# Two-block transformer kernel on one core: stick-breaking outputs kept features first, both output norms applied as per-token factors in the output product, and half units between the attention's iterations

## The chip, the cores and the metric

The kernel runs on one core of one Trainium2 chip. The metric is the device time of one execution in microseconds (us), lower is better. The engines that matter are TensorE (PE in the profile; PEld are its weight loads), VectorE (DVE) and ScalarE (ACT). SyncE (SP) issues the weight transfers.

## The reference, cut to what matters

`x` has 512 tokens of width 1024. A first block mixes and feeds forward, then a second block (three attentions, gates, 16 experts) follows, which the change doesn't touch. The part of the first block that it touches:

```
u = rms_norm(x, norm_mix) @ w_in           # 2560 columns: lru_x, lru_g, q, k, v of 512 each
y_lru = gelu(lru_g) * rg_lru(conv(lru_x))  # [512 tokens, 512 features]
# stick-breaking attention, 8 heads of 64, query blocks of 128:
z = q @ k.T / 8;  mask = key < query
att = where(mask, exp(log_sigmoid(z) + suffix sums of log_sigmoid(-z)), 0)
y_att = att @ v                            # [512, 512]
y = concat(rms_norm(y_lru, norm_lru_out), rms_norm(y_att, norm_att_out))
x = x + y @ w_out                          # w_out [1024, 1024]
h2 = rms_norm(x, norm_ffn) ...             # the feed-forward follows
```

`rms_norm(y, g)` is `y * rsqrt(mean over the 512 features of y*y + 1e-6) * g`: a factor per token and a gain per feature.

## The kernel before, in words

`plan` is a list of steps, written in Python before anything is emitted. Every engine walks the same list and emits its share of each step, so the list's order is the order of each engine's queue, and semaphores count finished steps.

A weight product is a *unit*. SP loads 1 MB of weights into one half of `RAW`; ACT rounds them to `WH` (L1161), DVE takes the remainder to `WL` (L1342), each for unit u+1 while unit u is at work, and PE forms three products (hi*hi, lo*hi, hi*lo) for each of 8 (or 4) slices of the contraction. Such a product has one record in the trace. Units of mode "F" give features first (128 features by 512 tokens; L1643 to L1645), "T" tokens first (L1660 to L1662), "wide" 512 columns of output for four token tiles (L1651 to L1653). Their results go to the banks `LIN`; while attention runs, to two of them in turn, and a product into the second of the two waits for the sigmoids of the iteration it stands in (`e_ab`). ACT or DVE evacuates. `out_half(j, h)` is a wide unit: columns 512*j of `w_out`, rows of the LRU half (h=0) or of the attention half (h=1), 4 slices, four results, each added to `X` by DVE.

The attention "stick" has 16 iterations (4 pairs of heads by 4 query blocks). With i counted from 0, iteration i of a pair has 4, 3, 2, 1 key tiles for i mod 4 = 0, 1, 2, 3. The order in iteration i:

- S(i): two score products into PSUM (L1690); ACT takes two sigmoids of each (`SK`, `SE`, L1203 and L1204, four instructions).
- W(i): DVE masks the last tile of `SE`, scans `SK` along the keys, multiplies into `PB` (L1396, L1397, L1403).
- T(i-1): PE transposes `PB` (L1773). It waits for W(i-1), and for the copies C(i-2).
- C(i-1): ACT and DVE copy the transposes into `PT` (L1314, L1584; DVE has a share only with 3 or 4 key tiles). It waits for O(i-2), since `PT` is single.
- O(i-2): PE multiplies by the values into the bank `PV` (L1792): `PT` is the stationary operand, 64 columns of `VT` move. DVE copies `PV` into `YT`, tokens first (L1437).
- fill(i): whatever the table `fill` has for i, whole units above all.

S(i) sits ahead of T(i-1) on PE, so what PE has to do between S(i) and T(i) is T(i-1), O(i-2), fill(i) and S(i+1).

The norm of `y_lru` (features first, `YL_`) is spread over the attention: `lsquare` (ACT squares), `lnorm` (PE sums the squares with a matrix of ones, L1755, which gives every token's sum on all 128 partitions; ACT takes the root, L1284; DVE the reciprocal of 128 x 512, L1566, and the product with `YL_`, L1567), `lsplit` (the gain and the split into `XH`, `XL`, L1289 and L1573). A root needs another activation table than a sigmoid, so tables are loaded ahead of it and behind it. The norm of `y_att` comes after the attention: `rms` on `YT` (ACT squares with sums, L1247; root; DVE reciprocal and scaling, L1512), PE transposes (L1739), ACT and DVE apply the gain and split (L1233, L1501). `out_half(1, 0)` covers the `rms`, and the two units of the attention half follow.

Of the kernel before, what the change touches and what calls it, by code (L numbers as in the profile page):

```python
# [85 lines left out]
def build(nc, x, w_in, w_out, w_ffn_in, w_ffn_out, mem, w_in2, w_memkv, w_branch, w_out2, w_router,  # L86
# [49 lines left out]
    YT = at("YT", R0 + 40, [P, TT, 512])  # L136
# [66 lines left out]
    def vec(c, n=1):  # L203
# [6 lines left out]
               ms_hi ms_lo saved band0 band1 x2h x2l xal lgp lgs afp af top ixp icc rcp pn ohi t1 wrp xt_ps xtA xtD lgc lg2""".split()  # L210
# [88 lines left out]
    def attention(kind, heads, halves, fill, after):  # L299
# [41 lines left out]
        def o_step(i):  # L341
            mine[i].o = add("O", dict(pv=1, o=1, ohi=int(kind != "stick")), a=mine[i])
# [33 lines left out]
    def queries(j):  # L376
        return unit(win, 1024 + UC * j, KT, "F", "scaled", dst=lambda r: QT[:, 2 * j + r, :], scale=0.125)

    def keys(j):
        return unit(win, 1536 + UC * j, KT, "F", "copy", dst=lambda r: KTT[:, 2 * j + r, :])  # L380

    def vals(j):
        return unit(win, 2048 + UC * j, KT, "T", "copy", dst=lambda r: VT[:, 2 * r:2 * r + 2, UC * j:UC * j + UC])
# [10 lines left out]
    def norm_sum():  # L394
        st = add("lnorm", dict(res=1, evA=1, yn=1), after=qkv[1], who=["act"], r0=len(results))
        take_banks(st)

    def out_half(j, h):
        return unit(w_out[0], 512 * j, 4, "wide", "accX", src=("xl", "xa")[h], row0=512 * h)
# [119 lines left out]
    SRC = {"x": (XH, XL), "xl": (XH[:, 0:4], XL[:, 0:4]), "xa": (XH[:, 4:8], XL[:, 4:8]), "m": (MH, ML), "a": (AH, AL), "y0": (YH2, YL2), "y1": (YH3, YL3),  # L519
# [625 lines left out]
    def _(act):  # L1145
# [73 lines left out]
        for st in plan:  # L1219
# [14 lines left out]
            elif k == "rms":  # L1234
                for t in range(TT):
                    if "ready" in st.kw:
                        act.wait_ge(st.kw["ready"][t], 16)
                    elif st.src is YT:
                        wait(act, "o", st.at)
                    else:  # L1240
                        wait(act, "evD", st.at, TT - 1 - t)
                    if st.dst is YT:
                        dump = PB[:, t // 2, t % 2, :]
                    else:
                        dump = (XN[:, t, :] if t == TT - 1 or "ready" in st.kw else
                                (PB[:, t, :, :] if t < 2 else PT[:, :, :]).rearrange("p a b -> p (a b)"))
# [35 lines left out]
            elif k == "lnorm":  # L1282
                act.wait_ge(s["res"], st.r0 + 1)
                A(RBC[:, :], LIN[lin_of[st.r0]][:, :], ACT.Sqrt, scale=1.0 / 512, bias=eps6).then_inc(s["evA"], 1)  # L1284
                act.preload_act_table_set("sigmoid_and_others")
            elif k == "lsplit":
                act.wait_ge(s["yn"], 1)
# [28 lines left out]
            elif k == "O" and st.a.att != "stick":  # L1316
# [14 lines left out]
    def _(dve):  # L1331
# [13 lines left out]
        def evacuate(st, now):  # L1345
            for r in now.now:
# [505 lines left out]
```

## Time and profile before

| what | us |
|---|---|
| median of 3 runs | 1761.27 (1758.52 to 1764.08) |
| the profiled execution, whole | 1763.7 |
| its span, first to last instruction | 1761.5 |
| from the first score product of "stick" to the last attention output | 130.78 to 271.45 |
| from there to the last product of the attention half of `w_out` | to 307.94 |
| PE busy over the span | 1588.2 (90%) |

A row of windows reads: from:to and its length, then busy time and instructions of PE, PEld, DVE, ACT and POOL, PEclk, the share of the DMA engines and GB/s. A row of the timeline reads: start, duration, engine, line, operation, out<-in, shape, count, and in brackets how long the engine was idle before it and what ended that. An f32 matmul has two records, a product of split weights (fp32r) one: T(i) with 4 key tiles is 8 transposes. PEclk is the clock granted to TensorE in a stretch, as a share of full speed, so 0.50 is 1.2 GHz and 1.00 is 2.4 GHz.

### The profile page before, as it was taken

How to read it: one execution, taken by the hardware profiler on the slowest of the kernel's cores; microseconds unless marked ns; L12 is line 12 of the kernel's file. 1: busy time of each engine (PE TensorE's matmuls, PEld its weight loads, DVE VectorE, ACT ScalarE, POOL GpSimd, SP SyncE). 2: the span in 40 equal slices, each digit the busy share in tenths (PEclk: the TensorE clock that was granted, in tenths of full speed). 3: DMA queues.
4: the chain of work that ended last, by engine and by line, in shares of the span. 5: the costliest groups of instructions: out<-in, count | busy, mean ns of one | idle time of the engine just before them, and what ended most of it. 6: DMA issues, size and time to landing. Idle time of an engine off the chain costs nothing.

```text
span 1761.5 us, 20656 instructions
## 1 busy us (share of the span) xinstructions
PE 1588.2 (90%) x7932; PEld 1116.3 (63%) x7932; DVE 741.6 (42%) x1094; ACT 523.2 (30%) x818; POOL 112.1 (6%) x152
## 2 busy tenths in 40 slices
PE   5989799999999998998999989996699999999894
PEld 4677687887887877987667768775333534434331
DVE  4455554434334335384535444346432232322335
ACT  4253433422222223224444434222021222112211
POOL 3000000000000000031102111001500000000000
PEclk9998789999999999999999999998799999999998
DMA  6212022333332323533202112328299999999993
GB/s 196 72 52 68 25 73 72 96 96 96 94 96 93 92 81 120 144 95 97 73 28 70 48 49 72 122 94 340 81 379 416 410 418 415 415 421 417 415 418 135
DMA packets 145095, 307.90 MB, mean 175 GB/s; under 512 B 7328, under 2 KB 98848, under 8 KB 128624
## 3 DMA queue, kind: packets, MB, share of 16 engines
q1 hardware_dynamic: 138992, 294.67, 45.3%
q0 software_dynamic: 3024, 9.10, 1.6%
q10 hardware_dynamic: 2992, 2.91, 0.6%
q8 instruction: 62, 1.02, 0.2%
q14 instruction: 25, 0.20, 0.0%
HBM read 300.36 MB, written 4.56 MB: 173 GB/s over the span
## 4 chain that ended last, share of the span: by engine, by line
PE 76%; DMA 9%; DVE 8%; issue 3%; ACT 3%; ACTq 1%; SPq 0%; DVEq 0%
PE bank L1009 12%; PE bank L1643 11%; PE bank L1644 10%; PE bank L1645 10%; DMA RING<-w_gu 4%; PE bank L1651 4%; PE bank L1652 4%; PE bank L1653 4%; DMA RING<-w_down 4%; PE bank L1690 2%; PE bank L982 2%; PE bank L1773 2%; PE bank L1020 2%; PE bank L983 2%; PE bank L1660 1%
## 5 line engine op out<-in xcount | busy, mean ns | idle before, releaser
L1643 PE MATMUL bank<-XH,WH 128*128 128x512 f32 x768 | 304.9, 397 | 6.5 <-DVE WL L1342 4.5
L1644 PE MATMUL bank<-XL,WH 128*128 128x512 f32 x768 | 301.4, 392 | 0.0
L1645 PE MATMUL bank<-XH,WL 128*128 128x512 f32 x768 | 301.2, 392 | 0.0
L1342 DVE TENSOR_TENSOR WL<-RAW,WH 128x2048 fp32r<-128x2048 f32 (+1 forms) x91 | 194.1, 2133 | 152.6 <-ACT WH L1161 152.6
L1009 PE MATMUL bank<-RING,XS 128*64 128x512 f32 x488 | 222.7, 604 | 12.9 <-DMA RING<-w_gu 8.2
L1010 PE MATMUL bank<-RING,XS 128*64 128x512 f32 x496 | 226.3, 604 | 0.0
L1161 ACT ACTIVATE WH<-RAW 128x2048 fp32r<-128x2048 f32 (+1 forms) x91 | 161.8, 1778 | 151.7 <-PE bank L1653 126.4
L1643 PEld LDWEIGHTS bank<-XH,WH 128*128 128x128 f32 x768 | 145.9, 190 | 40.1 <-DVE WL L1342 5.3
L1645 PEld LDWEIGHTS bank<-XH,WL 128*128 128x128 f32 x768 | 145.7, 190 | 30.8
L1644 PEld LDWEIGHTS bank<-XL,WH 128*128 128x128 f32 x768 | 145.9, 190 | 29.8 <-issue 0.2
L1009 PEld LDWEIGHTS bank<-RING,XS 128*64 128x64 f32 x488 | 63.7, 138 | 144.4 <-issue 140.0
L1020 PE MATMUL bank<-RING,HT 128*64 128x512 f32 x512 | 118.8, 599 | 13.9 <-DMA RING<-w_down 13.7
L890 DVE TENSOR_TENSOR GUS<-bank,LOH 64x512 f32<-64x512 f32 x64 | 39.6, 675 | 136.4 <-ACT LOH L791 136.4
L791 ACT ACTIVATE LOH<-bank 64x512 f32<-64x512 f32 x64 | 32.8, 589 | 215.1 <-PE bank L1010 215.1
L879 DVE TENSOR_TENSOR X<-bank,X 128x512 f32<-128x512 f32 x64 | 44.0, 688 | 117.9 <-PE bank L983 117.9
L1020 PEld LDWEIGHTS bank<-RING,HT 128*64 128x64 f32 x512 | 34.1, 136 | 90.6 <-issue 50.0
L1364 DVE TENSOR_TENSOR X<-bank,X 128x512 f32<-128x512 f32 x72 | 49.2, 690 | 81.1 <-PE bank L1653 78.9
L1651 PE MATMUL bank<-WH,AH 128*128 128x512 f32 x176 | 69.6, 395 | 7.9 <-issue 6.9
L1660 PE MATMUL bank<-WH,XH 128*128 128x256 f32 x224 | 65.7, 293 | 8.0 <-DVE WL L1342 6.5
L1652 PE MATMUL bank<-WL,AH 128*128 128x512 f32 x176 | 69.0, 392 | 0.0
L1653 PE MATMUL bank<-WH,AL 128*128 128x512 f32 x176 | 69.0, 392 | 0.0
L1773 PE MATMUL bank<-CST,PB 128*128 128x128 f32 x304 | 49.0, 299 | 20.7 <-DVE PB L1403 16.0
(300 smaller groups left out, 2488.7 us busy)
## 6 DMA issues: line engine op xcount, KB each, us to landing
RING<-w_gu SPq DMA_DIRECT2D x123, 1024.0 KB, 13.6
RING<-w_down SPq DMA_DIRECT2D x64, 1024.0 KB, 11.8
RAW<-w_in SPq DMA_DIRECT2D x66, 512.0 KB, 4.8
RAW<-w_ffn_in SPq DMA_DIRECT2D x44, 512.0 KB, 4.7
RAW<-w_ffn_out SPq DMA_DIRECT2D x20, 512.0 KB, 4.4
RAW<-w_out SPq DMA_DIRECT2D x16, 512.0 KB, 4.6
RAW<-w_branch SPq DMA_DIRECT2D x24, 256.0 KB, 3.2
ONCE<-w_gu SPq DMA_DIRECT2D x5, 1024.0 KB, 16.2
```

Of the source, the lines that this page charges most:

```text
L1009: T.matmul(GU[b][0:CAP, :], XS[:, k - 1, 2 * i + e, :], before[:, f], start=k == 1, stop=k == 7)
L1010: ins = T.matmul(GU[b][CAP:P, :], XS[:, k, 2 * i + e, :], slot[:, f], start=k == 1, stop=k == 7)
L1020: ins = T.matmul(YB[e][h][k * CAP:k * CAP + CAP, :], HT[:, e, 2 * r + k, :], slot[:, D * k + 512 * h:D * k + 512 * h + 512], start=r == 0, ...
L1161: A(WH[:, u % 2, :n], RAW[:, u % 2, :n], ACT.Copy).then_inc(s["w_hi"], 1)
L1342: V.tensor_tensor(WL[:, u % 2, :n], RAW[:, u % 2, :n], WH[:, u % 2, :n].bitcast(F32), ALU.subtract).then_inc(s["w_lo"], 1)
L1643: T.matmul(bank[:, :st.nt], wh[:, k, c], hi, start=k == 0, stop=False)
L1644: T.matmul(bank[:, :st.nt], wh[:, k, c], lo, start=False, stop=False)
L1645: ins = T.matmul(bank[:, :st.nt], wl[:, k, c], hi, start=False, stop=k == st.K - 1)
L1651: T.matmul(bank[:, :], hi, wh[:, k, :], start=k == 0, stop=False)
L1652: T.matmul(bank[:, :], hi, wl[:, k, :], start=False, stop=False)
L1653: ins = T.matmul(bank[:, :], lo, wh[:, k, :], start=False, stop=k == st.K - 1)
L1773: ins = T.transpose(TR[kt // 2][:, c:c + P], PB[:, st.a.n % 2, j, kt * P:kt * P + P], ident)
```

## The change

- The stick attention's output product has `VT` (64 columns) as the stationary operand and 128 queries of `PT` moving, so that it comes out features first, two heads in one 128 x 128 tile. ACT squares it into `SQ`, and applies the gain of `norm_att_out` while it rounds it to `YAH`; DVE takes the remainder to `YAL`. `YT`, its `rms` and its transposes are gone.
- The sums of squares per token are products with one column of ones: `square_sum` for the attention, one per iteration, emitted behind the *next* iteration's output product; 16 of them in `lnorm` instead of four of 512 columns. A new step `asum` sums the columns behind the last iteration and makes the four factors per partition.
- `lnorm` no longer scales `YL_`; its root and reciprocal have 4 columns. The factors (`ST[:, 32:36]` and `ST[:, 36:40]`) are applied by DVE where it adds the results of `out_half` to `X`.
- The three units for the second half of q, k and v go in halves, one half per iteration 0 to 5; `memk` 0 and 1, the split, and both LRU halves of `w_out` have other places in `fill`.

```diff
     def o_step(i):
-        mine[i].o = add("O", dict(pv=1, o=1, ohi=int(kind != "stick")), a=mine[i])
+        mine[i].o = add("O", dict(pv=1, o=1, ohi=1, sq=int(kind == "stick")), a=mine[i])
...
-    fill = {0: [lambda: queries(1)], 2: [lambda: keys(1)], 4: [lambda: qkv.append(vals(1))],
-            6: [lambda: add("lsquare", dict(ysq=1), after=qkv[1])], 7: [norm_sum],
-            9: [lambda: add("lsplit", dict(yhi=4, ylo=4), after=qkv[1])], 10: [memk(0)], 12: [memk(1)],
-            14: [lambda: out_half(0, 0)]}
-    last = attention("stick", 4, 4, fill, lambda i: qkv[i // 8])
-    rms(YT, YT, 512, after=last)
-    out_half(1, 0)
-    tx(YT, XH[:, 4:8], XL[:, 4:8], 4, TT, scale=V_GATT, feeds="xa")
+    q1, k1, v1 = (halves(f(1, False)) for f in (queries, keys, vals))
+    fill = {0: [q1[0]], 1: [q1[1]], 2: [k1[0]], 3: [k1[1]], 4: [v1[0]], 5: [lambda: qkv.append(v1[1]())],
+            6: [lambda: add("lsquare", dict(ysq=1), after=qkv[1]), memk(0)], 7: [norm_sum],
+            8: [lambda: add("lsplit", dict(yhi=4, ylo=4), after=qkv[1])], 9: [memk(1)],
+            11: [lambda: out_half(0, 0)], 13: [lambda: out_half(1, 0)]}
+    stick_last = attention("stick", 4, 4, fill, lambda i: qkv[i // 8])
+    add("asum", dict(ass=1, asq=1, arc=1, rat=1), after=stick_last)
     for j in range(2):
         out_half(j, 1)
...
# ACT, step O
+                act.wait_ge(s["pv"], st.a.n + 1)
+                A(SQ[:, :], src, ACT.Square).then_inc(s["sq"], 1)
+                A(hi, src, ACT.Copy, scale=vec(V_GATT + st.a.h)).then_inc(s["ohi"], 1)
# DVE, step O
-                V.tensor_copy(YT[...], PV[...]).then_inc(s["o"], 1)
+                V.scalar_tensor_tensor(lo, src, vec(V_GATT + a.h), hi.bitcast(F32), ALU.mult,
+                                       ALU.subtract).then_inc(s["o"], 1)
# PE, step lnorm
-                for c in range(4):
-                    ins = T.matmul(LIN[lin_of[st.r0]][:, :], ones, YSQ[:, c, :], start=c == 0, stop=c == 3)
+                for t in range(TT):
+                    for c in range(4):
+                        ins = T.matmul(LIN[lin_of[st.r0]][:, t:t + 1], YSQ[:, c, t * P:t * P + P], ones[:, 0:1],
+                                       start=c == 0, stop=c == 3)
# DVE, step lnorm
-                link(V.reciprocal(RBC[:, :], RBC[:, :]))
-                V.tensor_tensor(YL_[:, :, :], YL_[:, :, :], RBC[:, :].unsqueeze(1).to_broadcast([P, 4, S]), ...)
+                V.reciprocal(ST[:, 32:36], ST[:, 32:36]).then_inc(s["lrs"], 1)
# DVE, evacuation of out_half
+                    if "part" in st.kw:
+                        dve.wait_ge(s["rat" if st.kw["part"] else "lrs"], 1)
+                        c = 32 + 4 * st.kw["part"] + r
+                        V.scalar_tensor_tensor(xs, shaped(st, bank), ST[:, c:c + 1], xs, ALU.mult, ALU.add)...
# PE, step O of "stick", behind its products
+                if a.att == "stick" and a.n:
+                    ins = square_sum(atts[a.n - 1])
                 ins.then_inc(s["pv"], 1)
```

On PE, from the sums of `lnorm` (fill 7) to the next unit. Before, the scores of iterations 8, 9 and 10 follow (512, 384 and 256 columns), with their transposes and output products between:

```order
L1755 MATMUL bank<-YSQ,CST 128x512 [waits evD,evA,ysq]
L1755 MATMUL bank<-YSQ,CST 128x512 x3
L1690 MATMUL bank<-KTT,QT 128x512 [waits tx_hi,sig,tx_lo,e_ab,evD,evA]
L1690 MATMUL bank<-KTT,QT 128x512 [waits e_ab,evD,evA]
L1773 MATMUL bank<-CST,PB 128x128 [waits tx_hi,tx_lo,ptD,sig,ptA,p]
L1773 MATMUL bank<-CST,PB 128x128
L1792 MATMUL bank<-VT,PT 128x64 [waits o,ptD,ptA]
L1792 MATMUL bank<-VT,PT 128x64 x3
```

Now the sums are 16 short products, and each output product has a product with `SQ` behind it:

```order
L1785 MATMUL bank<-CST,YSQ 128x1 [waits evD,evA,ysq]
L1785 MATMUL bank<-CST,YSQ 128x1 x15
L1713 MATMUL bank<-KTT,QT 128x512 [waits tx_hi,sig,tx_lo,e_ab,evD,evA]
L1713 MATMUL bank<-KTT,QT 128x512 [waits e_ab,evD,evA]
L1807 MATMUL bank<-CST,PB 128x128 [waits tx_hi,tx_lo,ptD,sig,ptA,p]
L1807 MATMUL bank<-CST,PB 128x128
L1822 MATMUL bank<-PT,VT 64x128 [waits o,ptD,ptA]
L1822 MATMUL bank<-PT,VT 64x128 x3
L1719 MATMUL bank<-CST,SQ 128x1 [waits sq]
```

Behind these rows both have the scores of iteration 9 and the transposes and output of 8 and 7; the next unit, `memk`, stood behind O(8) and S(10), and now stands right behind O(7).

On PE, the end of the attention. Before, the last transposes and outputs ran into the LRU unit `out_half(1, 0)`:

```order
L1773 MATMUL bank<-CST,PB 128x128
L1792 MATMUL bank<-VT,PT 128x64 [waits o,ptD,ptA]
L1792 MATMUL bank<-VT,PT 128x64 x3
L1792 MATMUL bank<-VT,PT 128x64 [waits o,ptD,ptA]
L1792 MATMUL bank<-VT,PT 128x64
L1651 MATMUL bank<-WH,XH 128x512 [waits evA,evD,tx_lo,e_ab,ylo,w_lo]
```

Now they run into `asum` and the first unit of the attention half, whose wait on `o` is the split of the last output:

```order
L1807 MATMUL bank<-CST,PB 128x128
L1822 MATMUL bank<-PT,VT 64x128 [waits o,ptD,ptA]
L1822 MATMUL bank<-PT,VT 64x128 x3
L1719 MATMUL bank<-CST,SQ 128x1 [waits sq]
L1822 MATMUL bank<-PT,VT 64x128 [waits o,ptD,ptA]
L1822 MATMUL bank<-PT,VT 64x128
L1719 MATMUL bank<-CST,SQ 128x1 [waits sq]
L1719 MATMUL bank<-CST,SQ 128x1 [waits sq,o]
L1674 MATMUL bank<-WH,YAH 128x512 [waits evA,tx_lo,evD,o,e_ab,ylo,w_lo]
```

No unit moved across the products of the attention's last iterations except `out_half(1, 0)`, which stood behind them and is now in iteration 13.

## Rows read from the trace of the kernel before

**Rows 1.** The page: busy time by engine, and the chain that ended last

```profile
PE 1588.2 (90%) x7932; PEld 1116.3 (63%) x7932; DVE 741.6 (42%) x1094; ACT 523.2 (30%) x818; POOL 112.1 (6%) x152
...
PE 76%; DMA 9%; DVE 8%; issue 3%; ACT 3%; ACTq 1%; SPq 0%; DVEq 0%
```

**Rows 2.** Windows: attention, what follows it, and 90 us of a later attention

```profile
130.78:271.21 140.43, 122.60 (x649) 101.21 (x649) 77.45 (x142) 52.51 (x101) 0.00 (x0) 0.82 0.16 53
271.21:307.94 36.73, 36.38 (x164) 29.95 (x164) 18.82 (x24) 15.56 (x23) 0.00 (x0) 0.96 0.29 87
810.00:900.00 90.00, 80.14 (x453) 59.36 (x451) 44.20 (x113) 40.71 (x96) 13.03 (x28) 0.96 0.21 62
```

**Rows 3.** Waits of PE from 130 to 308: total, times, longest

```profile
PE bank L1773 <- DVE PB L1403: 16.0, 5, 6.3
```

**Rows 4.** Windows: the stretches at the lower clock

```profile
147.90:158.10 10.20, 9.37 (x33) 8.39 (x34) 5.50 (x11) 2.40 (x2) 0.00 (x0) 0.50 0.00 0
188.80:202.50 13.70, 13.64 (x48) 10.26 (x47) 4.46 (x15) 4.95 (x8) 0.00 (x0) 0.50 0.00 0
209.30:226.40 17.10, 12.39 (x56) 11.58 (x57) 15.25 (x29) 6.70 (x12) 0.00 (x0) 0.50 0.00 0
246.90:257.10 10.20, 9.50 (x34) 8.47 (x35) 5.70 (x11) 2.40 (x2) 0.00 (x0) 0.50 0.00 0
270.80:274.20 3.40, 3.40 (x11) 2.82 (x11) 0.29 (x1) 2.39 (x8) 0.00 (x0) 0.51 0.00 0
```

**Rows 5.** Timeline of PE: waits, and what the work after them takes

```profile
150.03 3.52 PE L1792 MATMUL bank<-VT,PT 128*128 128x64 f32 x16
...
213.90 1.97 PE L1773 MATMUL bank<-CST,PB 128*128 128x128 f32 x8 [6.25 <-DVE PB L1403]
...
268.97 1.00 PE L1792 MATMUL bank<-VT,PT 128*128 128x64 f32 x8
```

**Rows 6.** Timeline of PE at the full clock: scores, transposes, a later attention's output

```profile
130.78 1.13 PE L1690 MATMUL bank<-KTT,QT 64*128 64x512 f32 x4 [1.09 <-ACT VT L1190]
143.79 1.10 PE L1773 MATMUL bank<-CST,PB 128*128 128x128 f32 x8
...
936.41 1.09 PE L1788 MATMUL bank<-PT,KVT 128*64 128x128 f32 x16
```

**Rows 7.** Windows: one F unit, one T unit, `memk`, the two last wide units

```profile
131.84:142.94 11.10, 11.10 (x50) 8.93 (x49) 6.14 (x7) 4.47 (x6) 0.00 (x0) 1.00 0.47 160
171.09:182.76 11.67, 11.67 (x98) 11.54 (x97) 6.33 (x8) 3.81 (x6) 0.00 (x0) 1.00 0.28 91
235.84:241.75 5.91, 5.91 (x48) 5.78 (x49) 5.24 (x7) 2.32 (x3) 0.00 (x0) 1.00 0.00 0
285.91:307.94 22.03, 22.03 (x98) 18.25 (x99) 11.07 (x12) 7.98 (x10) 0.00 (x0) 1.00 0.35 96
```

**Rows 8.** Line L1755 and timeline of ACT and DVE: the norm of `y_lru`

```profile
L1755 PE MATMUL bank<-YSQ,CST x8: 592/1061/1167, 197.4 to 203.0; 128*128 128x512 f32 x8
...
203.60 0.69 ACT L1284 ACTIVATE RBC<-bank,CST 128x512 f32<-128x512 f32 x1 [4.02 <-PE bank L1755]
204.31 1.28 ACT L1285 ACT_TABLE_LOAD   x1
...
204.32 3.35 DVE L1566 RECIPROCAL RBC<-RBC 128x512 f32<-128x512 f32 x1 [6.40 <-ACT RBC L1284]
```

**Rows 9.** Timelines of ACT and DVE: from S(0) to its weights

```profile
131.97 0.60 ACT L1203 ACTIVATE SK<-bank 128x512 f32<-128x512 f32 x1 [0.35 <-PE bank L1690]
...
135.82 1.27 DVE L1403 TENSOR_TENSOR PB<-SE,SC 128x512 f32<-128x512 f32 x2
```

**Rows 10.** Timelines of PE, ACT and DVE: the end of the attention and the transposes

```profile
283.65 1.91 PE L1739 MATMUL bank<-CST,YT 128*128 128x128 f32 x16
...
270.07 0.38 ACT L1314 ACTIVATE PT<-bank 128x256 f32<-128x256 f32 x1 [1.45 <-PE bank L1792]
...
271.49 0.29 DVE L1437 COPY YT<-bank 128x128 f32<-128x128 f32 x1 [1.18 <-PE bank L1792]
```

More of the change, by code:

```diff
@@ L135, in build @@
     VT = at("VT", R0 + 32, [P, TT, 512])
[L136 removed]
+    YAH = at("YAH", R0 + 40, [P, 4, S], F32R)
     FG = at("FG", R0 + 16, [P, 2, S])
@@ L374, in build, with made, queries, keys @@
     add("lgate", dict(gmm=8, sig=8), after=lgu)
[L376 to L383, printed above, removed]
+    def made(args, kw, now):
+        return unit(*args, **kw) if now else (args, kw)
+    def queries(j, now=True):
+        return made((win, 1024 + UC * j, KT, "F", "scaled"), dict(dst=lambda r: QT[:, 2 * j + r, :], scale=0.125), now)
+    def keys(j, now=True):
+        return made((win, 1536 + UC * j, KT, "F", "copy"), dict(dst=lambda r: KTT[:, 2 * j + r, :]), now)
+    def vals(j, now=True):
+        return made((win, 2048 + UC * j, KT, "T", "copy"),
+                    dict(dst=lambda r: VT[:, 2 * r:2 * r + 2, UC * j:UC * j + UC]), now)
     qkv = []
@@ L394, in norm_sum, with halves @@
     def norm_sum():
-        st = add("lnorm", dict(res=1, evA=1, yn=1), after=qkv[1], who=["act"], r0=len(results))
+        st = add("lnorm", dict(res=1, evA=1, lrs=1), after=qkv[1], who=["act"], r0=len(results))
         take_banks(st)
     def out_half(j, h):
-        return unit(w_out[0], 512 * j, 4, "wide", "accX", src=("xl", "xa")[h], row0=512 * h)
-    fill = {0: [lambda: queries(1)], 2: [lambda: keys(1)], 4: [lambda: qkv.append(vals(1))],
-            6: [lambda: add("lsquare", dict(ysq=1), after=qkv[1])], 7: [norm_sum],
-            9: [lambda: add("lsplit", dict(yhi=4, ylo=4), after=qkv[1])], 10: [memk(0)], 12: [memk(1)],
-            14: [lambda: out_half(0, 0)]}
-    last = attention("stick", 4, 4, fill, lambda i: qkv[i // 8])
-    rms(YT, YT, 512, after=last)
-    out_half(1, 0)
-    tx(YT, XH[:, 4:8], XL[:, 4:8], 4, TT, scale=V_GATT, feeds="xa")
+        return unit(w_out[0], 512 * j, 4, "wide", "accX", src=("xl", "ya")[h], row0=512 * h, part=h)
+    def halves(part):
+        return in_two(*part[0], **part[1])
+    q1, k1, v1 = (halves(f(1, False)) for f in (queries, keys, vals))
[5 more added lines that the diff above has]
+    add("asum", dict(ass=1, asq=1, arc=1, rat=1), after=stick_last)
     for j in range(2):
@@ L1283, in _ @@
                 act.wait_ge(s["res"], st.r0 + 1)
-                A(RBC[:, :], LIN[lin_of[st.r0]][:, :], ACT.Sqrt, scale=1.0 / 512, bias=eps6).then_inc(s["evA"], 1)
+                A(ST[:, 32:36], LIN[lin_of[st.r0]][:, 0:TT], ACT.Sqrt, scale=1.0 / 512, bias=eps6).then_inc(s["evA"], 1)
                 act.preload_act_table_set("sigmoid_and_others")
             elif k == "lsplit":
-                act.wait_ge(s["yn"], 1)
+                wait(act, "res", st.after.end)
                 for c in range(4):
@@ L1315, in _ @@
                 ins.then_inc(s["ptA"], 1)
-            elif k == "O" and st.a.att != "stick":
+            elif k == "asum":
+                act.wait_ge(s["asq"], 1)
+                A(ST[:, 36:40], ST[:, 124:128], ACT.Sqrt, scale=1.0 / 512, bias=eps6).then_inc(s["arc"], 1)
+            elif k == "O" and st.a.att == "stick":
+                src, hi, _ = features(st.a)
+                act.wait_ge(s["pv"], st.a.n + 1)
+                A(SQ[:, :], src, ACT.Square).then_inc(s["sq"], 1)
+                A(hi, src, ACT.Copy, scale=vec(V_GATT + st.a.h)).then_inc(s["ohi"], 1)
+            elif k == "O":
                 src, hi, _ = features(st.a)
@@ L1609, in product @@
             wait(pe, "ylo", st.at)
+            if st.src == "ya":
+                wait(pe, "o", stick_last.end)
             if st.evac == "branch":
@@ L1690, in scores, with square_sum @@
             T.matmul(o, q, kk, start=True, stop=True).then_inc(s["qk"], 1)
+        def square_sum(a):
+            c = 256 + 4 * a.h + a.qt[0]
+            pe.wait_ge(s["sq"], a.n + 1)
+            return T.matmul(PV[:, c:c + 1], SQ[:, :], ones[:, 0:1], start=True, stop=True)
         def values(a, j, kt):
@@ L1781, in _ @@
                 wait(pe, "o", st.at)
-                for kt in range(a.nkt[0] if a.att != "stick" else 0):
+                for kt in range(a.nkt[0]):
                     first, last = kt == 0, kt == a.nkt[0] - 1
```

49 lines of the change are left out of this document (25 added, 24 removed).

## Prediction

> **What bounds the kernel now.** I read the page first: PE is busy for 90% of the span and makes up 76% of the chain that ended last [rows 1]. So a change counts if it shortens PE's work, PE's idle time, or the time PE spends at the lower clock. I then read windows around the place of the change. The attention takes 140.43 us, of which PE is busy for 122.60, at a mean granted clock of 0.82; then come 36.73 us at 0.96 to the last product of `out_half(1, 1)` [rows 2]. Together that is 177.2 us, 130.78 to 307.94, and this is the stretch I redo. Next the waits: five times the transposes T wait for DVE's weights `PB`, 16.0 us in all, the longest 6.3 [rows 3]. With the start (1.1 before a bank is free, 0.8, 0.5 and 0.35 at the end, read off the timeline) PE is idle for about 18 us. Last the clock: the windows split at its changes show five stretches at the lower level, 54.6 us in all (10.2 + 13.7 + 17.1 + 10.2 + 3.4) [rows 4]. Each of the four long ones begins within two us of the start or end of a wait for `PB`, and what runs there takes about twice as long: an output product with 4 key tiles has 16 records in 3.52 us at the lower level, one with 2 tiles 8 records in 1.00 us at the full one [rows 5].
>
> **What PE has to do, at the full clock, before and after.** Per pair of heads (4, 3, 2, 1 key tiles):
>
> - Scores: 1.06 us from the start with 512 columns to the next instruction (1.13 with its tail [rows 6]), falling with the columns to 0.42; 2.96 per pair. Transposes: 8 in 1.10 with the tail, so 0.137 each, 20 per pair: 2.7 [rows 6]. Neither changes.
> - Output: before, 2 records and 0.25 us per product [rows 5], 20 products: 5.0. After, the form is that of the later attention, 16 records in 1.09 for 8 products [rows 6], 0.13 to 0.14 each: 2.6. The two heads go to different halves of the columns there too. Four pairs: 9.6 us less.
> - `square_sum`: this trace has no product with one moving column. The nearest row is the output product of before, which moves 64 columns through 128 stationary ones at 0.25 us; from below, the 0.13 of the features-first form. I take 0.25, since the stationary operand has 128 columns in both: 16 x 0.25 = 4.0 us more (2.1 from below).
> - `lnorm`: 4 products of 512 columns, 0.59 us per record where the clock was up (8 records [rows 8]), about 3.5 us at the full clock; they took 6.2 at the lower one. After: 16 x 0.25 = 4.0 (2.1 from below).
> - Units: a unit of q or k 11.1, of v 11.67, `memk` 5.9, a wide one 11.0 [rows 7]: 22.2 + 11.7 + 11.8 + 44.1 = 89.8, the same before and after. A half costs half; all its operands are there.
> - The transposes of `YT` (1.91 [rows 10], 2.3 with the wait): gone.
>
> Sum before: 4 x 10.7 + 3.5 + 89.8 + 1.9 = 138.0. With 18 idle, 177.2 - 138.0 - 18 = 21 us are left for the lower clock, which fits 54.6 us of it, part of them idle. Sum after: 4 x (2.96 + 2.7 + 2.6 + 1.0) + 4.0 + 89.8 = 130.9, so 7 less.
>
> The Trainium skill (TensorE: Matmul & The Clock Gate, LDWEIGHTS) gives a weight load by its columns over 1.2, that is 107 ns for 128 columns, whatever moves. By that and the two records per product, the 32 short products would cost 32 x 2 x 0.107 = 6.8 us, an estimate, where the rows gave 8.0.
>
> **Idle time after.** T(i) needs W(i). From the end of S(0), 131.91, ACT's four sigmoids and DVE's chain run to 137.09 [rows 6, 9]: 5.2 us with 4 key tiles, less with fewer. Between S(i) and T(i) PE has T(i-1), O(i-2), fill(i), S(i+1).
>
> - Iterations 0 to 6 now all have 5.5 to 6 us of unit there, where 1, 3 and 5 had none. The waits at T(1) and T(5) go; 4 of the 5 waits share 16.0 - 6.3 = 9.7, so 2.4 each, 5 us in all. In iteration 1 the half unit writes the second bank and has to wait for the sigmoids of S(1): 0.6.
> - Iteration 8 has no product of a unit, and 4 key tiles. From the end of `lnorm`: ACT's root of 4 columns (below the 0.69 of now), the table 1.28 [rows 8], the sigmoids from 1.65 on, the first pair done at 2.7, then 3.9 on DVE (131.97 + 1.1 to 137.09 [rows 9]): 6.6. PE has S(8), T(7), O(6), S(9), together 3.1. Wait 3.5, instead of 6.25 [rows 5]: what is gone is DVE's reciprocal (3.35 [rows 8]) with the product behind it, which stood ahead of W(8). `memk(1)`, right behind O(7), needs the split of `lsplit`, which DVE ends at about 9.6; PE gets there at 8.3 to 9.5, so at most 1.3 more, and none if the clock is low.
> - Iteration 12 has 4 key tiles and an empty fill; in the order of before `memk(1)` covered it. S(12) end + 5.2, less T(11), O(10) and S(13), 2.0: wait 3.1.
> - Iterations 10 and 14 (2 key tiles, empty fill): between nothing and the 2.4 that such a wait costs now. I take 1.0 each; DVE's queue, with the split in front of W(9), is late for T(10).
> - The tail. `PV` is single, and now ACT squares it and copies it and DVE subtracts before the next output product may write it: three instructions of 0.3 us by the size of the row of `YT` [rows 10], and C, 0.38 [rows 10], stands ahead of them on ACT. From the end of an output product to the start of the next some 1.4 to 1.7 us, where one copy of 0.29 was. Elsewhere the fills hide it; behind O(13), O(14) and O(15) nothing does, since the first attention unit waits for the last split. The stretch from O(13) to that unit is 5.2 us with 2.0 of work: 3.2 idle. The reciprocal of `asum` ends before the unit's first result (2.7 us), so it hides.
>
> Sum: 0.6 + 3.5 + 1.0 + 3.1 + 1.0 + 3.2 = 12.4, against 18.
>
> **The clock.** Before, the waits of 2.4 to 6.3 us cost 21 us in four long stretches. Three places are left that look alike: T(8), T(12), and the tail. The first two cost what the stretches of 10.2 us cost, where 3.52 instead of 2.0 and a unit of 13.5 instead of 11 add up to some 4; so 4 and 3. The tail runs into 11 us of unit: 3. Sum 10, against 21. That iterations 0 to 7 hold the full clock I take from the later attention, which has half units in its iterations and this form of output product, and is at 0.96 over 90 us [rows 2].
>
> **The sum.** 130.9 + 12.4 + 10 = 153.3, against 177.2: 23.9 us less. Behind 307.94 nothing is changed and PE stays the bound, so the whole shift should reach the end. 1763.7 - 23.9 = 1739.8 for the profiled execution; the median of the runs lies 2.4 below it, so **1737.5**. DVE's evacuation with a factor is as long as the addition was (both read PSUM and `X`, 128 x 512) and ends before the next result.
>
> **The rivals.** A measurement here can tell about 0.3%, 5 us.
>
> - *The clock falls for longer in the second half.* Fills 8, 10, 12, 14 are empty, and waits of about 1 us alternate with short products. For it: at the end of the attention two waits of under a us, among such products, were followed by 3.4 us at the lower level [rows 4]. If the clock stays low from T(8) to the first attention unit, but for the wide units, the S, T, O of iterations 8 to 15 (19 us) and half of three units (14) run at half speed, while waits hide a third: 22 us instead of 10. Time 1750. The Trainium skill (TensorE: Matmul & The Clock Gate, A second HAM failure mode) tells of such a kernel, with micro-idles between groups of products, whose clock kept switching; the trace agrees in that row. Chance 20%.
> - *Only T(8) and T(12) cost clock, and both less; the short products cost 0.13.* Loss 4 instead of 10, 4 us less work: 1728. Against it: each wait of over 2 us before had its stretch. Chance 15%.
> - *The clock stays low through the attention, and the kernel is slower.* The products of the new form are shorter, and each 11 us unit, which brought the clock back before, is cut in two. All attention work outside the last two units is 109 us; the change loses once the added loss passes 24 us over my 10, that is once some 68 us run low. With all of it low the loss is 109, and the time about 1761 + (130.9 + 12.4 + 109 - 177.2 - some 15 of waits that shrink against doubled work) = 1821. Against it: rows 2. Chance 3%.
> - *Nothing comes of it*: waits for weights take the place of the waits for `PB`, as DVE's and ACT's splits queue behind the new instructions. For it: ACT gets 32 instructions more, some 9 us. Against it: ACT is busy for 52.5 of the 140 us and DVE for 77 [rows 2], and a weight is split two iterations ahead. Chance 3%.
> - My forecast, within 1731 to 1745: 59%.
>
> **How the numbers follow.** The forecast holds 59%; the low-clock case and the cheap case take the range to 1750 and 1728 with spread of their own. With 1726 to 1750 some 2 in 10 is left out. Faster by over 0.3%: 59 + 20 + 15, 94%. Within: 3. Slower: 3.
>
> **What would show it.** In the windows, PE's stretch from the first score to the last attention product at about 153 us. `square_sum` and `lnorm` at 0.25 us a product. No wait of over a us before iteration 8, and the clock at 1.00 there. A wait of 3 to 4 at T(8) and at T(12), and lower clock behind each. In the tail some 3 us in waits for `YAL` and `PT`. I am wrong if the low stretches sum to over 40 us, if waits for `WL` appear, or if what is won here is given back behind 307.94.

## The result, and the profile after

| | median us | ratio to before, 95% interval |
|---|---|---|
| before, 9 runs | 1761.79 | |
| changed, 9 runs (1743.49 to 1753.11) | 1750.93 | 0.9921, 0.9900 to 0.9942 |

By the medians the kernel is 11 us faster, by the ratio 14 (10 to 18), where 24 were forecast; the median of 1750.9 stands a hair above the upper end of the range of 1726 to 1750. The nine times of the changed kernel fall into two groups, three of 1743.5 to 1745.1 and six of 1750.7 to 1753.1; the profiled one, 1751.76, is of the slower group. The page after, to be read beside [rows 1], hardly differs:

```profile
PE 1581.3 (90%) x7972; PEld 1103.8 (63%) x7972; DVE 738.5 (42%) x1086; ACT 524.9 (30%) x838; POOL 111.8 (6%) x152
```

The windows tell more (the columns are those of [rows 2]). First the stretch from the first score to the first product behind the attention half of `w_out` (before: 130.78 to 307.77, 177.0 us), then the rest, then the three stretches at the lower clock within the first:

```profile
129.66:288.12 158.46, 146.71 (x849) 116.08 (x850) 88.71 (x158) 70.03 (x144) 0.00 (x0) 0.90 0.21 67
288.12:1750.00 1461.88, 1337.02 (x6677) 907.70 (x6675) 588.79 (x863) 397.28 (x623) 96.87 (x124) 0.97 0.52 194
191.00:208.10 17.10, 15.68 (x68) 11.67 (x68) 12.42 (x21) 11.20 (x21) 0.00 (x0) 0.50 0.06 24
235.40:242.20 6.80, 6.80 (x24) 5.27 (x23) 5.12 (x9) 2.82 (x4) 0.00 (x0) 0.50 0.00 0
262.70:269.50 6.80, 6.60 (x17) 5.25 (x18) 3.43 (x5) 3.16 (x3) 0.00 (x0) 0.50 0.01 3
```

The stretch went from 177.0 to 158.5 us, the time in it at the lower clock from 54.6 [rows 4] to 30.7. So 18.5 us were won there. But what follows took 1453.7 before (1761.5 - 307.8) and takes 1461.9 now: 8 us were lost there again, in code that the change doesn't touch.

The waits of PE in the stretch, in the form of [rows 3]:

```profile
PE bank L1807 <- DVE PB L1422: 6.6, 4, 3.1
PE bank L1822 <- DVE YAL L1457: 1.9, 2, 1.4
PE bank L1713 <- ACT VT L1200: 1.1, 1, 1.1
PE bank L1719 <- DVE YAL L1457: 1.0, 1, 1.0
PE bank L1807 <- issue: 0.8, 1, 0.8
PE bank L1666 <- ACT SE L1214: 0.8, 1, 0.8
```

The waits for `PB` fell from 16.0 to 6.6. The new ones, for `YAL`, are those of the tail. Here is PE's timeline where the sums of `lnorm` (L1785) run into the scores of iteration 8:

```profile
187.96 0.38 PE L1719 MATMUL bank<-CST,SQ 128*128 128x1 f32 x2
188.20 4.44 PE L1785 MATMUL bank<-CST,YSQ 128*128 128x1 f32 x32
192.57 2.08 PE L1713 MATMUL bank<-KTT,QT 64*128 64x512 f32 x4
```

and the window from the first sum to the fall of the clock:

```profile
188.20:191.00 2.80, 2.80 (x27) 2.80 (x27) 1.32 (x6) 2.30 (x4) 0.00 (x0) 1.00 0.87 238
```

PE was busy all the while, and yet the lower clock begins at 191.0, among the sums: the 32 records start at 188.20, and the scores behind them take 2.08 us, where they took 1.13 in [rows 6]. The wait at T(8) comes only at 198.4, seven us later.

### The profile page after: what moved, and what is told of

Its sections match the earlier page's. It is cut to its first block, busy times and chain, and to the rows that moved or that the text cites. A ratio compares the mean times of both kernels' runs of the same rounds, so it can differ in the third digit from the quotient of the medians.

```text
span 1750.0 us, 20743 instructions
## 1 busy us (share of the span) xinstructions
PE 1581.3 (90%) x7972; PEld 1103.8 (63%) x7972; DVE 738.5 (42%) x1086; ACT 524.9 (30%) x838; POOL 111.8 (6%) x152
## 4 chain that ended last, share of the span: by engine, by line
PE 77%; DVE 8%; DMA 8%; ACT 3%; issue 3%; ACTq 1%; SPq 0%; DVEq 0%
PE bank L1019 12%; PE bank L1666 11%; PE bank L1667 10%; PE bank L1668 10%; PE bank L1674 4%; PE bank L1675 4%; PE bank L1676 4%; DMA RING<-w_down 3%; DMA RING<-w_gu 3%; PE bank L1713 2%; PE bank L992 2%; PE bank L1030 2%; PE bank L1807 2%; PE bank L993 2%; PE bank L1822 2%
## 5 line engine op out<-in xcount | busy, mean ns | idle before, releaser
L1019 PE MATMUL bank<-RING,XS 128*64 128x512 f32 x488 | 225.3, 611 | 11.9 <-DMA RING<-w_gu 7.2
L1020 PE MATMUL bank<-RING,XS 128*64 128x512 f32 x496 | 228.9, 610 | 0.0
L1019 PEld LDWEIGHTS bank<-RING,XS 128*64 128x64 f32 x488 | 64.6, 139 | 145.0 <-issue 140.6
L889 DVE TENSOR_TENSOR X<-bank,X 128x512 f32<-128x512 f32 x64 | 44.0, 688 | 122.6 <-PE bank L993 122.6
L1370 DVE TENSOR_TENSOR FP<-bank,FG 128x512 f32<-128x512 f32 x22 | 15.2, 691 | 121.7 <-PE bank L1668 121.7
L1020 PEld LDWEIGHTS bank<-RING,XS 128*64 128x64 f32 x496 | 65.6, 139 | 0.0
```

The lines of the kernel that those rows point to most:

```text
L1019: T.matmul(GU[b][0:CAP, :], XS[:, k - 1, 2 * i + e, :], before[:, f], start=k == 1, stop=k == 7)
L1020: ins = T.matmul(GU[b][CAP:P, :], XS[:, k, 2 * i + e, :], slot[:, f], start=k == 1, stop=k == 7)
```

## The experiments

The stretch is again from the first score of "stick" to the first product of the unit behind the attention half of `w_out`; "rest" is the span after it. Medians are of all runs of a kernel, ratios are to the kernel before with their 95% intervals; stretch, lower clock and rest are of the one profiled run. The changed kernel's own profile is the yardstick: 158.5 stretch, 30.7 of it at the lower clock.

**Two parts of the change, each alone.** First the changed kernel with the fills of before:

```diff
-    fill = {0: [q1[0]], 1: [q1[1]], 2: [k1[0]], 3: [k1[1]], 4: [v1[0]], 5: [lambda: qkv.append(v1[1]())],
-            6: [lambda: add("lsquare", dict(ysq=1), after=qkv[1]), memk(0)], 7: [norm_sum],
-            8: [lambda: add("lsplit", dict(yhi=4, ylo=4), after=qkv[1])], 9: [memk(1)],
-            11: [lambda: out_half(0, 0)], 13: [lambda: out_half(1, 0)]}
+    fill = {0: [lambda: queries(1)], 2: [lambda: keys(1)], 4: [lambda: qkv.append(vals(1))],
+            6: [lambda: add("lsquare", dict(ysq=1), after=qkv[1])], 7: [norm_sum],
+            9: [lambda: add("lsplit", dict(yhi=4, ylo=4), after=qkv[1])], 10: [memk(0)], 12: [memk(1)],
+            14: [lambda: out_half(0, 0)]}
...
+    out_half(1, 0)
```

> The changed kernel, but the fills stand as before (whole units for q, k, v in iterations 0, 2, 4, then memk in 10 and 12, one LRU half of w_out in 14, the other behind the attention). It keeps features first, the short sums and the factors. The stretch from the first score to the last attention product of w_out was 177.2 us before and 158.5 after. Theory A (the order of the fills is the larger part, since it takes the waits for PB and the lower clock behind them): the stretch is at about 167 us, the waits of 3 us at T(1), T(5) and T(13) are back and a stretch at the lower clock follows each. Theory B (the products themselves are the larger part): the stretch is at 162 us or below.

Stretch 161.6, 27.3 at the lower clock, median 1760.9, ratio 0.9978 (0.9952 to 1.0005). The waits for `PB` are back, 11.6 us in five, but the stretches at the lower clock are short now, 3.4 or 6.8 us each. The stretch came out as B said, in this one profile; the times of the ten runs are hardly told from before.

Then the kernel before with nothing but the half units of q, k and v:

```diff
-    fill = {0: [lambda: queries(1)], 2: [lambda: keys(1)], 4: [lambda: qkv.append(vals(1))],
+    fill = {0: [q1[0]], 1: [q1[1]], 2: [k1[0]], 3: [k1[1]], 4: [v1[0]], 5: [lambda: qkv.append(v1[1]())],
             6: [lambda: add("lsquare", dict(ysq=1), after=qkv[1])], 7: [norm_sum],
...
```

> The kernel before, with one thing of the change: the second-half units of q, k and v are cut in halves and stand in iterations 0 to 5; all else (YT, its norm, lnorm, the other fills) as before. Theory A: the waits at T(1) and T(5), 6 us, go, and with them two stretches at the lower clock (10.2 and some of 13.7 us); the stretch goes from 177.2 to about 166. Theory B (half units cost as much as they save, by their own starts and waits for the second bank): above 173.

Stretch 161.3, 23.9 at the lower clock, median 1755.7, ratio 0.9939 (0.9913 to 0.9966). A's waits went, 16.0 down to 10.0 for `PB`, and more than two low stretches with them, so that the stretch is 5 us shorter than A had it. The windows over the stretch, of this kernel and then of the one with the old fills:

```profile
130.04:291.38 161.34, 146.18 (x809) 120.47 (x809) 96.15 (x166) 68.38 (x124) 0.00 (x0) 0.93 0.21 66
```

```profile
130.03:291.58 161.55, 144.59 (x848) 115.31 (x849) 89.38 (x158) 68.98 (x144) 0.00 (x0) 0.92 0.21 66
```

In these profiles either part alone gives 15 to 16 of the 18.5 us, and less time at the lower clock than the whole change has (23.9 and 27.3 against 30.7). That looks as if both lived on the same low stretches and so didn't add. It isn't shown: each is one profile, and below the attention code of before, unchanged, has one stretch of 163.4 us by a kinder clock alone. How the 18.5 us divide between the order of the units and the products stays open. Both profiles also show the dear way described below, with a rest of 1465.7 and 1466.8 (in the order of the windows), which is why their whole times gain less than their stretches; 4 to 5 us of these rests are beyond the dear way's 1461.5, and nothing here says why.

**What brought the clock down at 191.** The sums of `lnorm` with 128 columns of ones moving instead of one:

```diff
-                        ins = T.matmul(LIN[lin_of[st.r0]][:, t:t + 1], YSQ[:, c, t * P:t * P + P], ones[:, 0:1],
+                        ins = T.matmul(LIN[lin_of[st.r0]][:, t * P:t * P + P], YSQ[:, c, t * P:t * P + P], ones[:, :],
...
```

(ACT's root then reads each 128th column of the result.)

> The changed kernel, but each of the 16 sum products of lnorm moves 128 columns of ones instead of one. A product is bound by its stationary operand, so it takes the 0.27 us that it took. In the changed kernel the lower clock sets in while these products run, with PE busy and no wait for 5 us. Theory C (the clock fell since short products move too little, busy or not): with 128 columns the lower clock sets in only behind the wait at T(8) or not at all, and the scores of iteration 8 (2.08 us) are back at 1.1; the wait at T(8) grows from 1.4 towards 3.5; the stretch shrinks by 2 to 4 us. Theory D (it fell for something that lies before them, or at a moment of its own): nothing changes, 158 to 159 us.

PE's timeline, then its windows up to the change of clock and through the low stretch:

```profile
187.29 3.82 PE L1785 MATMUL bank<-CST,YSQ 128*128 128x128 f32 x32
191.04 1.13 PE L1713 MATMUL bank<-KTT,QT 64*128 64x512 f32 x4
```

```profile
187.30:196.20 8.90, 7.47 (x54) 5.43 (x53) 3.85 (x11) 7.32 (x15) 0.00 (x0) 1.00 0.36 119
196.20:206.40 10.20, 8.57 (x40) 7.92 (x41) 10.20 (x17) 6.16 (x12) 0.00 (x0) 0.50 0.01 2
```

C holds. The 16 products end sooner (3.8 us against 4.4) since none of them runs at the lower clock, the scores of iteration 8 are back at 1.13, and the clock falls at 196.2, in the wait at T(8), which has grown from 1.4 to 3.05. Stretch 156.0, 20.5 at the lower clock, 2.5 us less. The median, 1746.3 of 4 runs, has the ratio 0.9909 (0.9876 to 0.9942), which doesn't tell it from the changed kernel; the trace does.

One profile could be chance, but the others agree. The sums with one column stand in six profiles: in four, all with the changed kernel's order of units, the clock fell 2.3 to 2.8 us into them; in the kernel with the old fills at their end (193.5); in the kernel of the next experiment 1.4 us behind them (192.6), with PE busy since their start. The sums with 128 columns stand in three, and in each the clock held through them and fell in a wait of PE or just behind one, 4 to 5 us after the last sum. At the full clock the 16 products cost nearly the same either way, here one column (all halves, next) and 128 (all together, further on):

```profile
187.53 3.63 PE L1790 MATMUL bank<-CST,YSQ 128*128 128x1 f32 x32
```

```profile
189.47 3.74 PE L1791 MATMUL bank<-CST,YSQ 128*128 128x128 f32 x32
```

**The waits that were left.** All units of the attention in halves, also `memk` and the LRU halves of `w_out`; `in_two` and `rest` take the second half of four results too:

```diff
-            6: [lambda: add("lsquare", dict(ysq=1), after=qkv[1]), memk(0)], 7: [norm_sum],
-            8: [lambda: add("lsplit", dict(yhi=4, ylo=4), after=qkv[1])], 9: [memk(1)],
-            11: [lambda: out_half(0, 0)], 13: [lambda: out_half(1, 0)]}
+            6: [lambda: add("lsquare", dict(ysq=1), after=qkv[1]), m0[0]], 7: [m0[1], norm_sum],
+            8: [m1[0], lambda: add("lsplit", dict(yhi=4, ylo=4), after=qkv[1])], 9: [m1[1]],
+            10: [w0[0]], 11: [w0[1]], 12: [w1[0]], 13: [w1[1]]}
...
```

> The changed kernel, with memk and the LRU halves of w_out cut in halves too: memk 0 in iterations 6 and 7 (the second half ahead of lnorm), memk 1 in 8 and 9 (the first half ahead of lsplit), w_out in 10 to 13, nothing in 14. If waits and the lower clock behind them are what is left of the gain that was forecast: the waits at T(8), T(10) and T(12), 5.6 us, go but for under 1 us, the clock stays up from iteration 8 to 13 but for the sums, and the stretch goes from 158.5 to about 149. If the clock falls by the short products alone, the waits go and the lower clock stays: about 153. The tail, 3.7 us of waits for YAL and PT, stays in both.

Stretch 149.2, 17.1 at the lower clock, median 1735.5, ratio 0.9858 (0.9816 to 0.9900). The waits of PE:

```profile
PE bank L1812 <- DVE PB L1427: 2.6, 2, 1.5
PE bank L1671 <- ACT SE L1219: 2.0, 3, 0.8
PE bank L1827 <- DVE YAL L1462: 1.6, 2, 1.4
...
PE bank L1679 <- ACT SE L1219: 1.2, 2, 1.0
```

The 6.6 us for `PB` are 2.6, but the waits for the sigmoids, where a half unit stands in the second bank (`SE`), went from 1.0 to 3.2. So of the 9.3 us that the stretch lost, PE's idle time makes only 2.3 (11.7 to 9.4); the other 7.0 are busy time, with 13.6 us less at the lower clock. The forecast of 149 had 5 us of waits go; the clock fell once for 6.8 us at 192.6, behind the sums, so the size fits with a little luck. Part of the median's gain over the changed kernel is not from here: this profile has a rest of 1453.0, the cheap way below, where the changed kernel's has 1461.9. The same holds for the run with wide sums (1452.5).

**The 8 us that came back.** Ahead of the experts DVE makes the router's index tables while GpSimd scales `X`. In the changed kernel's second profile (1744.7 us) and third (1750.9) DVE's rows at this place are, first the one, then the other:

```profile
1227.09 3.43 DVE L852 TENSOR_TENSOR RB<-IDX,CST 16x256 f32<-16x256 f32 x2
1230.45 2.32 DVE L857 COPY VAL<-VAL 16x64 f32<-16x64 f32 x1
1232.69 0.18 DVE L858 CAST IDX<-IDU 16x64 f32<-16x64 uint32 x1
```

```profile
1226.39 5.62 DVE L852 TENSOR_TENSOR RB<-IDX,CST 16x256 f32<-16x256 f32 x2
1231.94 2.32 DVE L857 COPY VAL<-VAL 16x64 f32<-16x64 f32 x1
1234.19 2.37 DVE L858 CAST IDX<-IDU 16x64 f32<-16x64 uint32 x1
```

GpSimd's rows beside them:

```profile
1227.09 2.62 POOL L1135 TENSOR_TENSOR X<-X,LNR 128x1024 f32<-128x1024 f32 x1
1229.67 3.05 POOL L1134 TENSOR_TENSOR X<-X,LNR 128x1024 f32<-128x1024 f32 x1
```

```profile
1226.39 2.34 POOL L1135 TENSOR_TENSOR X<-X,LNR 128x1024 f32<-128x1024 f32 x1
1228.69 2.52 POOL L1134 TENSOR_TENSOR X<-X,LNR 128x1024 f32<-128x1024 f32 x1
```

A cast of 16 x 64 takes 0.18 or 2.37 us. In both DVE's product and GpSimd's start in the same hundredth of a us, and either GpSimd's is the longer one (2.62 for 2.34) or DVE's first product is (2.61 for 0.41). The first way costs 5.8 us from `RB` to the end of the cast, the second 10.2. I call them the cheap and the dear way. PE waits for the end of these tables, in the cheap way and in the dear:

```profile
1232.92 0.28 PE L965 MATMUL bank<-CST,VAL 16*128 16x16 f32 x1 [4.15 <-DVE IDX L858]
```

```profile
1236.62 0.28 PE L965 MATMUL bank<-CST,VAL 16*128 16x16 f32 x1 [6.35 <-DVE IDX L858]
```

The lower clock around this wait lasts longer with it, 30.7 us in the changed kernel's second profile and 37.5 in its first:

```profile
1208.30:1239.00 30.70, 8.32 (x26) 5.26 (x27) 25.59 (x53) 3.07 (x4) 29.90 (x13) 0.50 0.10 41
```

```profile
1208.10:1245.60 37.50, 10.63 (x37) 7.57 (x38) 30.07 (x53) 4.18 (x6) 30.54 (x13) 0.50 0.08 35
```

The Trainium skill (SBUF — State Buffer, SBUF: two separate sides) says that the two engines share one pair of ports, which a GpSimd instruction or a DVE instruction with two SBUF inputs or in a two-port mode locks for its whole length, whichever starts first. The trace agrees that one holds the other up, DVE's rows being up to 2.2 us longer than alone and GpSimd's 0.2 to 0.7. It doesn't show who was first: GpSimd's record starts 5 to 6 ns ahead of DVE's in both ways.

To take the race away, GpSimd starts its eight instructions once the tables are there; this was added to both kernels:

```diff
                 pool.wait_ge(s["x2l"], TT)
+                pool.wait_ge(s["top"], 2)
                 for t in range(TT):
```

> The kernel before, with one wait more on GpSimd: its eight instructions on X ahead of the experts (2.34 us each) start only when VectorE has made the index tables of the router. In the profile of the kernel before these two run side by side, and VectorE's product for RB of 16 x 256 takes 0.41 us there and 2.61 in the changed kernel, a cast of 16 x 64 takes 0.17 and 2.37. Theory P (the two engines hold each other up over SBUF, and which of two ways it goes is settled by some tens of ns in each run): the four small instructions take 0.1 to 1 us each, 2 to 7 us go from the gap before the experts, the lower clock there gets shorter than 30.7 us, and runs scatter less; time 1755 to 1758 against 1762 to 1764. Theory Q (X is then late for the experts, or the gap is filled by a transfer anyway): no change or slower.

> The changed kernel with the same wait on GpSimd. Theory P: the changed kernel has the dear way in its profile and in 6 of 9 runs (1750 to 1753, the others 1743 to 1745), so it gains more than the kernel before does: 7 to 10 us, to 1741 to 1743, with the two groups of times gone, and the distance between the two kernels with the wait is what their attention stretches differ by, 18 to 19 us. Theory Q: 1750 as it was, and the distance stays at 11 to 13.

The kernel before: 1758.8, ratio 0.9962 (0.9944 to 0.9981). The changed one: 1740.3, ratio 0.9866 (0.9840 to 0.9893), and its six runs lie within 6.4 us, none in a group of its own. Theory P holds: the small instructions are short, PE's wait of 4 or 6 us is gone and the lower clock there lasts 27.3 us. Only its forecast of less scatter failed for the kernel before (1745.5 to 1762.0, where the 17 runs of before beside it span 1757.2 to 1771.0). DVE in the changed kernel:

```profile
1224.57 1.28 DVE L852 TENSOR_TENSOR RB<-IDX,CST 16x256 f32<-16x256 f32 x2
1225.78 0.18 DVE L857 COPY VAL<-VAL 16x64 f32<-16x64 f32 x1
1225.88 0.17 DVE L858 CAST IDX<-IDU 16x64 f32<-16x64 uint32 x1
```

With the race gone, the two kernels are 1758.8 - 1740.3 = 18.5 us apart, where they were 11: what the stretches of the first two profiles differ by. The intervals of the two ratios leave this distance open by some 6 us either way, so the times alone don't prove it; the profiles do better, with a rest of 1451.9 and 1450.2, 1.7 us apart instead of 8.2. GpSimd's later end costs nothing that shows.

**All together, and the tail.** The halves, the wide sums and the late GpSimd in one kernel:

> All halves, the 128-column sums in lnorm and the late GpSimd together. If the short sums alone bring the clock down at 191 us, the stretch at the lower clock from 192.6 (6.8 us) goes, and the stretch is at 147 us instead of 149.2; with what GpSimd gives back 1728 to 1732. If the lower clock stays there with the wide sums, it was not the sums that brought it down.

Median 1732.7, ratio 0.9813 (0.9787 to 0.9839); stretch 148.4 where 147 was expected, 10.2 at the lower clock. The low stretch at 192.6 is gone; a short one of 3.4 us begins at 197.2, after a wait of 1.5 us for `SE`. Then the output of iteration 14 in another bank, with tiles of their own for the squares of 14 and 15 and the last three sums of squares in `asum`:

```diff
-                wait(pe, "o", st.at)
+                late = a.att == "stick" and a.n >= 14
+                wait(pe, "o", st.at, int(late))
+                into = PV
+                if late and a.n == 14:
+                    wait(pe, "evD", st.at)
+                    into = LIN[0]
...
-                if a.att == "stick" and a.n:
+                if a.att == "stick" and 0 < a.n < 14:
```

> The kernel with all halves, wide sums and late GpSimd, and a freer end of the attention: the output of iteration 14 goes to another bank, so that it need not wait for the split of 13, and the three last sums of squares stand behind the last output. If the chain through ACT and DVE is what the tail costs, the waits for YAL at the last two outputs (0.2 to 0.5 and 1.44 us) go and 1.5 to 2 us with them; the last wait (1.0) stays. If the products wait for the copies into PT in any case, under 0.7.

Median 1730.9, ratio 0.9811 (0.9783 to 0.9838). PE's tail without the other bank and with it:

```profile
249.12 0.41 PE L1813 MATMUL bank<-CST,PB 128*128 128x128 f32 x2 [0.79 <-issue]
249.98 0.66 PE L1828 MATMUL bank<-PT,VT 128*64 128x128 f32 x8 [0.44 <-DVE YAL L1463]
...
252.39 0.69 PE L1828 MATMUL bank<-PT,VT 128*64 128x128 f32 x4 [1.44 <-DVE YAL L1463]
...
255.06 0.77 PE L1680 MATMUL bank<-WH,YAH 128*128 128x512 f32 x1
```

```profile
246.89 0.63 PE L1819 MATMUL bank<-CST,PB 128*128 128x128 f32 x2 [0.79 <-issue]
...
249.12 0.70 PE L1839 MATMUL bank<-PT,VT 128*64 128x128 f32 x4 [0.54 <-ACT PT L1329]
250.84 1.44 PE L1729 MATMUL bank<-CST,SQ 128*128 128x1 f32 x6 [1.02 <-DVE YAL L1467]
252.14 0.77 PE L1684 MATMUL bank<-WH,YAH 128*128 128x512 f32 x1
```

The waits of 0.44 and 1.44 went and one of 0.54 for the copy came, 1.3 us less idle; but the lower clock sets in earlier here, so from T(15) to the unit it is 5.25 us instead of 5.94. A gain of 0.7 in this part of the trace, 0.1 over the stretch (148.3), nothing that the runs can tell.

**How much one profile says.** Each kernel was profiled twice more, unchanged:

> The kernel before, unchanged, for a second profile. Its attention code is also that of the run with the late GpSimd, whose stretch took 163.4 us with 17 us at the lower clock, where the first profile of before had 177.2 and 54.6. Theory R (the clock in this stretch goes differently in each run, since its waits are near what brings the clock down): the stretch lies between 163 and 177. Theory S (177 is the rule, the other run the exception): 174 to 178.

> The kernel before, unchanged, a third profile. As above: R 163 to 177, S 174 to 178. RB of 16 x 256 takes either 0.41 or 2.61 us, nothing between.

> The changed kernel, unchanged, for a second profile. The runs so far with its code in the stretch took 158.5 and, with GpSimd late, much the same. Theory R: it scatters less than before does, since fewer waits are left, 155 to 160. If it scatters as widely, the comparison of two single profiles says little of the stretch.

> The changed kernel, unchanged, a third profile. As above: 155 to 160 for the stretch; what follows it takes 1452 us where RB of 16 x 256 takes 0.41 and 1460 or more where it takes 2.61.

| profile | whole us | stretch | of it low | rest | way |
|---|---|---|---|---|---|
| before | 1763.7 | 177.0 | 54.6 | 1453.7 | cheap |
| before, second | 1761.0 | 175.7 | 51.2 | 1453.3 | cheap |
| before, third | 1764.7 | 175.6 | 51.2 | 1456.6 | cheap |
| before, GpSimd late | 1745.5 | 163.4 | 17.1 | 1451.9 | none |
| changed | 1751.8 | 158.5 | 30.7 | 1461.9 | dear |
| changed, second | 1744.7 | 158.4 | 30.7 | 1454.7 | cheap |
| changed, third | 1750.9 | 158.3 | 30.7 | 1461.5 | dear |
| changed, GpSimd late | 1738.3 | 158.2 | 30.7 | 1450.2 | none |

In the last column "none" means that DVE and GpSimd don't meet. S is the rule for before, and the changed kernel repeats itself to 0.3 us. But the attention code of the run with 163.4 us is that of before to the last instruction, and it spent 17 us at the lower clock instead of 51 to 55:

```profile
147.80:151.20 3.40, 3.40 (x14) 3.01 (x13) 0.93 (x3) 1.65 (x2) 0.00 (x0) 0.50 0.00 0
199.00:205.80 6.80, 3.43 (x16) 3.04 (x16) 6.80 (x13) 0.61 (x2) 0.00 (x0) 0.50 0.01 2
233.10:239.90 6.80, 6.80 (x28) 6.27 (x27) 2.61 (x7) 2.32 (x2) 0.00 (x0) 0.50 0.00 0
```

Its waits were no shorter: PE was idle for 20.4 us of the stretch (163.4 - 143.0), for 18.2 in the first profile. That run was the fastest of its twelve, by 7 us; the others were 1752.6 to 1762.0.

## Why the prediction was right, and where its sizes failed

- **The sum of PE's work** was set too low, 130.9. In the windows above PE is busy for 146.7 us of the stretch, 29.1 of them at the lower clock. The scores take 2.08 us there instead of 1.13, an output with 16 records in [rows 5] nearly 1.8 times its full-clock time; so the 29.1 would be about 16 at the full clock, and the work some 133.5, an estimate. Done alike for the kernel before (159.0 busy, 48.3 of them low) it gives some 136.7 for the forecast's 138.0. So the work fell by 3 us, not by 7. The prices of single products were near: 16 records of the output in 1.09, `lnorm` 3.63 at the full clock for 4.0. What was left out is what stands between them: `square_sum` takes 0.24 ahead of a unit, but 0.31 ahead of scores and 0.38 ahead of a wait (forecast 0.25); from the transposes to the output it is 0.37 us for two records, where the kernel before has 0.27; a half unit takes 5.66 instead of 5.55.
- **Idle time**, forecast 12.4: by the timeline 0.8 + 0.2 + 1.4 + 1.1 + 0.5 + 3.05 + 1.1 + 3.7 for the tail = 11.8. T(12) is 3.05 for 3.1, T(10) and T(14) 1.1 each for 1.0, the wait for the second bank 0.8 for 0.6. T(8) is 1.4 instead of 3.5, since the slow clock stretched what stands ahead of it. The tail is 3.7 (0.8, 0.4, 1.4, 1.0) for 3.2. One reading of before was wrong without consequence: the four lesser waits for `PB` are not 2.4 each, but 3.2, 2.9, 2.9 and, in the tail, 0.8.
- **The clock, forecast 10, cost about 13** (158.5 - 133.5 - 11.8), where it had cost 22 before. I let the clock fall where PE waits, at T(8), T(12) and in the tail. The last two did. The first fell before any wait, during the 16 one-column sums, and stayed down for 17.1 us. The run with wide sums shows that these sums brought it forward. Of the later attention, which I took as proof that short products are safe [rows 2], no product moves fewer than 128 columns.
- **"The whole shift should reach the end" failed** in the profiled run and, by their times, in most others; the prediction itself had named this as a sign of being wrong. 18.5 us were won in the profile and 8 given back, of which 4.4 in DVE's small instructions beside GpSimd's, the rest in lower clock (37.5 us of it ahead of the experts, 30.7 in the cheap way) and what follows. The code there is the same in both kernels; the three profiles of before had the cheap way, two of three of the changed one the dear way, and the late GpSimd brings the rests to within 1.7 us of each other. Whether the changed kernel meets the dear way more often, and why, stays open: of the 17 runs of before beside the late GpSimd's, eight took 1766.9 to 1771.0, more than any profiled one (1761.0 to 1764.7), and may have had it too.
- **The rivals**: the nearest in time was "the clock falls for longer in the second half" (1750). Its time came, but not its sum: the clock cost 13 us and not its 22, and the rest was lost behind the stretch. The cheap case and the slower one didn't come, nor did waits for `WL`.

So the mechanism held, fewer waits and less time at the lower clock behind them, and three sizes failed, all to the same side: the work by 3 us, the clock by 3, the rest by 8; the idle time was 0.6 better. The time near the range's end is no work of luck, for no two errors cancel; in the runs whose times fit the cheap way it is 1743 to 1745, well inside.

## What to carry to other kernels

A wait removed from the busiest engine may be worth more than twice its length through the clock: here the idle time fell by 6.5 us and the clock's cost by some 9. But the same waits can cost 22 us of clock in one run and 6 in another, so two edits that live on the same low stretch can't be counted on to add, and a stretch wants more than one profile. Ask of each new product how it runs where the clock might fall, not only how long it takes: sixteen sums over one column took 3.63 us, over 128 columns 3.74, and the short ones cost 2.5 us behind them. Count the joints between products of different forms as well as the products: a tenth of a us at each made up most of the 3 us by which the work was set too low. And before a gain early in the program is credited to the end, look for places further on where two engines start within hundredths of a us of each other: there the same code has two durations, and one profile shows one of them.

## What the runs showed of the hardware that I had not expected

- TensorE's clock went down to 1.2 GHz with PE busy: it fell 2.3 to 2.8 us into 16 f32 products with one moving column in the three profiles of the changed kernel (at 190.4 to 191.2) and in the one with the late GpSimd. With 128 moving columns it held there in all three profiles, and the 16 products took 3.7 to 3.8 us.
- The same attention code spent 51 to 55 us at the lower clock in three profiles, and 17 in a fourth, with no less idle time of PE: 12 to 14 us in one stretch.
- A DVE cast of 16 x 64 took 0.17 or 2.37 us beside GpSimd instructions of 2.34 us, and the choice, made at a start in the same hundredth of a us, moved the whole time by 6.2 us (1744.7 against 1750.9 in two profiles of one kernel).
